# Sample sequences planned four slots ahead of the attention heads, key turns beside the memory jobs

## The reference

```
# prompt: 8 heads of 64, 8 query blocks of 128, keys picked by an indexer (the kernel adds them as a bias)
s = einsum("bthd,btkhd->bthk", q, k_sel) * DH_ATT ** -0.5
p = softmax(where(valid, s, -inf));  o = einsum("bthk,btkhd->bthd", p, v_sel)
# sample: the same for 8 tokens of each of 8 sequences, keys and values from 16 cache pages of 128 rows,
# found by a page table, and from the 8 new tokens
# memory: 4 heads of 128 against 256 memory tokens, for the prompt and for each sample sequence
s = einsum("bthd,bmhd->bthm", qm, mk) * DH_MEM ** -0.5
p = softmax(s);  o = einsum("bthm,bmhd->bthd", p, mv)
```

## Time and profile before

| | |
|---|---|
| time before, median of 3 runs | 3330.24 us (3317.41 to 3333.93) |
| the profiled execution's own time | 3330.28 us |
| span of its trace | 3328.7 us |
| PE busy over the span | 3120.3 us (94%) |
| DVE / ACT / POOL busy | 1747.0 / 914.2 / 669.6 us (52 / 27 / 20%) |
| attention stage in the trace | 1714.5 to 2254.4 us |

### The profile page before, as it was taken

How to read it: one execution, slowest core, us unless ns; L and a number is a source line. 1 busy time by engine, 2 the same in 40 slices (tenths; PEclk the granted TensorE clock), 3 DMA queues, 4 the chain that set the end, 5 groups by cost and what they waited for, 6 DMA issues and landing times. The chain is left out here.

```text
span 3328.7 us, 51750 instructions
## 1 busy us (share of the span) xinstructions
PE 3120.3 (94%) x19690; PEld 2930.0 (88%) x19690; DVE 1747.0 (52%) x3049; ACT 914.2 (27%) x1616; POOL 669.6 (20%) x415
## 2 busy tenths in 40 slices
PE   7999999999998999999778878888999999999999
PEld 7999999999898999899656556567999999999998
DVE  6333333334589999998235555554735333333333
ACT  4111111113333332343334334332132111111111
POOL 2212222213533311233230000002112122222121
PEclk9999999999999999999879999898999999999999
DMA  3111111112222223122543355334431111111111
GB/s 112 45 38 50 44 44 44 44 38 68 73 79 77 79 80 89 39 76 82 165 152 133 115 163 193 115 112 145 153 90 44 40 44 46 43 44 44 44 38 67
DMA packets 256495, 265.47 MB, mean 80 GB/s; under 512 B 14575, under 2 KB 197458, under 8 KB 256334
## 3 DMA queue, kind: packets, MB, share of 16 engines
q1 hardware_dynamic: 250858, 254.61, 24.6%
q0 software_dynamic: 4128, 4.20, 0.4%
q10 hardware_dynamic: 1348, 4.49, 0.4%
HBM read 226.20 MB, written 37.05 MB: 79 GB/s over the span
## 5 line engine op out<-in xcount | busy, mean ns | idle before, releaser
L331 PE MATMUL bank<-h_hi,w_hi 128*128 128x362 f32 (+1 forms) x3384 | 1122.7, 332 | 28.8 <-DVE sg_ffn L513 8.3
L331 PE MATMUL bank<-h_lo,w_hi 128*128 128x362 f32 (+1 forms) x3384 | 1116.3, 330 | 0.0
L331 PE MATMUL bank<-h_hi,w_lo 128*128 128x362 f32 (+1 forms) x3384 | 1112.1, 329 | 0.0
L331 PEld LDWEIGHTS bank<-h_hi,w_hi 128*128 128x128 f32 x3384 | 640.4, 189 | 36.2 <-issue 21.4
L331 PEld LDWEIGHTS bank<-h_lo,w_hi 128*128 128x128 f32 x3384 | 640.9, 189 | 2.8
L331 PEld LDWEIGHTS bank<-h_hi,w_lo 128*128 128x128 f32 x3384 | 641.9, 190 | 0.0
L388 POOL TENSOR_TENSOR w_lo<-raw,w_hi 128x1024 fp32r<-128x1024 f32 x132 | 316.7, 2406 | 1273.3 <-ACT w_hi L483 1273.3
L550 DVE SCALAR_TENSOR_TENSOR x<-bank,x 128x362 f32<-128x362 f32 (+1 forms) x528 | 280.5, 535 | 213.4 <-PE bank L331 213.4
L331 PE MATMUL bank<-a_hi_ffn,w_hi 128*128 128x362 f32 (+1 forms) x1056 | 348.9, 330 | 4.3 <-DVE x L550 2.6
L331 PE MATMUL bank<-a_lo_ffn,w_hi 128*128 128x362 f32 (+1 forms) x1056 | 347.1, 329 | 0.0
L331 PE MATMUL bank<-a_hi_ffn,w_lo 128*128 128x362 f32 (+1 forms) x1056 | 345.7, 327 | 0.0
(11 more groups left out here) (371 smaller groups left out, 4175.6 us busy)
## 6 DMA issues: line engine op xcount, KB each, us to landing
raw<-in_w_ffn_in SPq DMA_DIRECT2D x88, 512.0 KB, 3.8
k_ring<-in_cache_k SPq DMA_DIRECT2D x128, 256.0 KB, 3.9
v_ring<-in_cache_v SPq DMA_DIRECT2D x128, 256.0 KB, 4.1
raw<-in_w_in SPq DMA_DIRECT2D x53, 512.0 KB, 4.9
raw<-in_w_ffn_out SPq DMA_DIRECT2D x44, 512.0 KB, 3.5
kept_g<-stage SPq DMA_DIRECT2D x24, 544.0 KB, 3.1
gate<-kept_g SPq DMA_DIRECT2D x24, 544.0 KB, 3.6
x<-x_kept SPq DMA_DIRECT2D x8, 544.0 KB, 4.6
```

What stands on the lines that cost most here:

```text
L331: mm = pe.matmul(out, left, right, start=(start and i == 0 and j == 0), stop=(stop and i == n - 1 and j == 2))
```

## The change

The sample work of slot k now runs at step k-4, so each sequence starts its slots 0 to 3 beside the four memory jobs of the head before, and the first sequence's slots 0 to 3 run ahead of all heads. The slots are regrouped: `sc 4`, the two memory `kt`, and a new entry `smax` (the maximum over ps, DVE's part of `soft`) stand together in slot 5 and run at step 1; `soft` (now ACT's exponential alone) and `msc` stand in slot 6, step 2. `scale` is gone: the division is folded into the copy of the pv result (`tensor_scalar` instead of `tensor_copy`). `oturn` comes one step later, ahead of the values. SP issues each value page five key pages later than before; its wait for pv and mpv then stands behind six key pages of the next sequence instead of one.

```
--- before.py
+++ after.py
@@ -2321,6 +2321,9 @@
     return cols.rearrange("p (b k) -> p b k", k=LT)[:, :, j]
 
+AHEAD = 4
+
+
 def attention_plan():
 
@@ -2336,9 +2339,9 @@
         [("sc", 0), ("kt", 4), ("kt", 5), ("kt", 6), ("kt", 7)],
         [("sc", 1), ("kt", 8), ("kt", 9), ("kt", 10), ("kt", 11)],
         [("sc", 2), ("kt", 12), ("kt", 13), ("kt", 14), ("kt", 15)],
-        [("sc", 3), ("sc", 4)],
-        [("soft",), ("kt", 16), ("kt", 17)],
-        [("scale",), ("msc",)],
+        [("sc", 3)],
+        [("sc", 4), ("kt", 16), ("kt", 17), ("smax",)],
+        [("soft",), ("msc",)],
         [("pt", 0), ("pt", 1), ("pt", 2), ("pt", 3), ("pt", 4)],
         [("pv",), ("mpt",)],
         [("mpv",), ("ot",)],
@@ -2358,29 +2361,32 @@
     n = len(jobs)
     add("stack", 0)
-    for s in range(n + 2):
-        if s < n:
+    for s in range(-AHEAD, n + 3):
+        if 0 <= s < n:
             add("scores", s)
-        if 0 <= s - 2:
+        if 0 <= s - 3:
+
+            kind, i, h = jobs[s - 3]
+            if kind == "att" and i == 4 and h % 2 == 1:
+                add("oturn", s - 3, 0)
+                add("oturn", s - 3, 1)
+            if kind == "mem" and i % 4 == 3:
+                add("oturn", s - 3, 0)
+        if 0 <= s - 2 < n:
             add("values", s - 2)
-            kind, i, h = jobs[s - 2]
-            if kind == "att" and i == 4 and h % 2 == 1:
-                add("oturn", s - 2, 0)
-                add("oturn", s - 2, 1)
-            if kind == "mem" and i % 4 == 3:
-                add("oturn", s - 2, 0)
         if 0 <= s - 1 < n:
             kind, i, h = jobs[s - 1]
             blocks = i + 1 if kind == "att" else 2
             for g in range(0, blocks, 4):
                 add("turn", s - 1, g, min(4, blocks - g))
-        if s < n:
-
+        if 0 <= s < n:
             add("exp", s)
-            for e in slots[s % 12]:
-                add(e[0], s // 12, *e[1:])
-            if s % 12 == 8 and s // 12 + 1 < H:
-                add("stack", s // 12 + 1)
+        if s + AHEAD < n:
+
+            for e in slots[(s + AHEAD) % 12]:
+                add(e[0], (s + AHEAD) // 12, *e[1:])
+        if s >= 0 and s % 12 == 8 and s // 12 + 1 < H:
+            add("stack", s // 12 + 1)
     return jobs, plan
 
@@ -2441,7 +2447,7 @@
     evicted = [sem("turn_act"), sem("turn_dve")]
     used5, freed5 = sem("used5"), sem("freed5")
-    s_scaled, tail_clear = sem("s_scaled"), sem("tail_clear")
+    tail_clear = sem("tail_clear")
     s_max, s_exp, s_inv, s_norm = sem("s_max"), sem("s_exp"), sem("s_inv"), sem("s_norm")
     m_max, m_exp, m_inv, m_norm = sem("m_max"), sem("m_exp"), sem("m_inv"), sem("m_norm")
@@ -2572,18 +2578,23 @@
                     if u < PAGES:
                         return I[name][0][bass.ds(page(u), 1)].rearrange("a p h d -> p (a h d)")
                     return I[mem_name][0][b].rearrange("(t p) h d -> t p (h d)", p=P)[u - PAGES]
-                for u in range(UP):
+                for u in range(UP + KR - 1):
                     n = b * UP + u
-                    if n >= KR:
-
-                        before = divmod(n - KR, UP)
-                        sp.wait_ge(turned, turn_of[("kt", *before)] + 1)
-                    sp.dma_start(k_ring[:, n % KR, :], source("cache_k", "cache_mem_k", u)).then_inc(k_in[n % KR], 16)
-                    if u == 0 and b >= 1:
+                    if u < UP:
+                        if n >= KR:
+
+                            before = divmod(n - KR, UP)
+                            sp.wait_ge(turned, turn_of[("kt", *before)] + 1)
+                        sp.dma_start(k_ring[:, n % KR, :], source("cache_k", "cache_mem_k", u)
+                                     ).then_inc(k_in[n % KR], 16)
+                    v = u - (KR - 1)
+                    if v < 0:
+                        continue
+                    if v == 0 and b >= 1:
                         sp.wait_ge(used5, use_of[("pv", b - 1)] + 1)
                         sp.wait_ge(used5, use_of[("mpv", b - 1)] + 1)
-                    sp.dma_start(v_ring[:, u, :], source("cache_v", "cache_mem_v", u)).then_inc(v_in[u // 8], 16)
-                    if u == 0:
+                    sp.dma_start(v_ring[:, v, :], source("cache_v", "cache_mem_v", v)).then_inc(v_in[v // 8], 16)
+                    if v == 0:
                         sp.dma_start(vn[:, :], O["new_v_sample"][0][b].rearrange("t h d -> t (h d)")
                                      ).then_inc(vn_in, 16)
@@ -2704,7 +2715,7 @@
                                        stop=(h == 3))
                     mm.then_inc(used5, 1)
                 elif kind == "pt":
-                    pe.wait_ge(s_scaled, s + 1)
+                    pe.wait_ge(s_exp, s + 1)
                     g = entry[2]
                     if g < 4:
                         for q in range(4):
@@ -2794,6 +2805,8 @@
                     act.copy(ps[:, g * 512:g * 512 + w], bank[5][:, 0:w]).then_inc(freed5, 1)
                 elif kind == "soft":
                     act.wait_ge(s_max, s + 1)
+                    if s >= 1:
+                        act.wait_ge(s_inv, s)
                     act.activation(ps[:, :], ps[:, :], ACT.Exp, bias=st[:, 0:1], accum_out=st[:, 1:2]).then_inc(s_exp, 1)
                 elif kind == "msc":
                     act.wait_ge(m_max, s + 1)
@@ -2850,25 +2863,23 @@
                         dve.wait_ge(turned, turn_of[("oturn", last_of["mem", s // 12 - 1], 0)] + 1)
                     dve.tensor_scalar(kept(s), bank[6][:, 0:w], rinv[:, s % 4:s % 4 + 1], None, ALU.mult
                                       ).then_inc(normed, 1)
-                elif kind == "soft":
+                elif kind == "smax":
                     dve.wait_ge(freed5, use_of[("sc", s, 4)] + 1)
                     if s >= 1:
                         dve.wait_ge(s_exp, s)
                     dve.tensor_reduce(st[:, 0:1], ps[:, :], AX.X, ALU.max, negate=True).then_inc(s_max, 1)
-                elif kind == "scale":
-                    dve.wait_ge(s_exp, s + 1)
-                    dve.reciprocal(st[:, 2:3], st[:, 1:2]).then_inc(s_inv, 1)
-                    dve.wait_ge(s_inv, s + 1)
-                    dve.tensor_scalar(ps[:, :], ps[:, :], st[:, 2:3], None, ALU.mult).then_inc(s_scaled, 1)
                 elif kind == "msc":
                     dve.wait_ge(used5, use_of[entry] + 1)
                     dve.tensor_reduce(st[0:32, 3:4], bank[5][0:32, 0:N_MEM], AX.X, ALU.max,
                                       negate=True).then_inc(m_max, 1)
                 elif kind == "pv":
+                    dve.wait_ge(s_exp, s + 1)
+                    dve.reciprocal(st[:, 2:3], st[:, 1:2]).then_inc(s_inv, 1)
+                    dve.wait_ge(s_inv, s + 1)
                     dve.wait_ge(used5, use_of[entry] + 1)
                     if s >= 1:
                         dve.wait_ge(turned, turn_of[("ot", s - 1)] + 1)
-                    dve.tensor_copy(os_[:, :], bank[5][:, 0:P]).then_inc(s_norm, 1)
+                    dve.tensor_scalar(os_[:, :], bank[5][:, 0:P], st[:, 2:3], None, ALU.mult).then_inc(s_norm, 1)
                     dve.wait_ge(s_norm, s + 1)
                     dve.sem_inc(freed5, 1)
                 elif kind == "mpv":
```

## The result

The change makes the kernel faster: 3296.43 us in the median of five runs (3292.73 to 3300.25) against 3325.57 for the kernel before in the same session, a ratio of 0.9915 with an interval of 0.989 to 0.9939. I had forecast 3325, with 0.55 on no change, and the time lies 2.6 us under my lower end of 3299.

The account below looks back on a forecast made before the run. PE's idle time and half clock in the attention stage were taken as the bound. Idle falls from 87 to 71.5 us, gaining 15.5; less 2.7 for the start and 8 for half clock leaves 5 off 3330.28: 3325 us, range 3299 to 3360.

Parts of the forecast that it names:

- What is removed: Attention stage: mks, o_sb, o_m, ps and key page waits go, save 3 us in the start; 64 us if nothing came.
- The stack gap: Steps 8 and 9: PE waits for DVE's copy behind the stack, 3.2 or 3.7 us, plus late exponential; 28 us in all.
- Steps 1 to 3: Copies queue behind the maximum over ps and the exponential; PE idles 21 us in all, against 34 us of old waits.
- steps 6 to 8: These steps lose their sample work; mot waits for a bank and values for a copy, 0.5 us each; 8 us.
- the key turns of step 8: Step 8: the first key turn waits 0.6 us for a copy, the third 0.3; 6 us over seven.
- steps 10 and 11: Key turns in these steps wait 0.35 us each, 5 us in all.
- the end: End of the stage: four last memory jobs with nothing beside them, 3.5 us.
- The start: Sequence 0 turns 16 pages before the first scores, 29.4 us into the stage; 16.6 us lost, a cost of 2.7 us.
- Half clock: PE at half clock behind gaps: 14 us today, 22 after from seven stack gaps and seven small ones; cost 8 us.
- the stack gap is hidden: Faster rival at steps 8 and 9: stack waits of only 1.0 us without loss of clock; 3299 us, chance 0.21.
- The clock halves in steps 8 to 11: Slower rival: old waits mostly stay gone but turns do not keep the clock up, costing 35 us; 3360 us, chance 0.22.
- the 0.8 that I had named: Sign for the half clock rival: mean granted clock below 0.8 in steps 9 to 11.

Follow-up runs that it names:

- e2: The changed kernel with the sample work back at its old steps, no slots ahead; 3254.4 us, 0.9781 of before.
- e10: The kernel before with 11 or 5 useless matmuls of 512 columns added to each mks gap; 3319.7 us, 0.999 of before.
- e11: The kernel of e2 with the stack's differences on GpSimd in place of DVE, as in e3; 3242.3 us, 0.9757 of before.
- e1: The kernel before with only the turns of the results (o_sb, o_m) one step later; 3303.1 us, 0.9929 of before.
- e6: The kernel of e2 with the old grouping of slots 4 to 6; 3293.8 us, 0.9912 of before.
- e12: The changed kernel with the sample work two slots ahead instead of four; 3296.7 us, 0.9925 of before.
- e9: The changed kernel with 14 useless matmuls of 512 columns added to each stack gap; 3290.7 us, 0.9896 of before.
- e3: The changed kernel with the stack's three differences on GpSimd in place of DVE; 3293.5 us, 0.9895 of before.
- e8: The kernel of e3 loading only 128 of 512 columns of each value page from the second sequence on; 3271.1 us, 0.9843 of before.

## Why the prediction was wrong

The stage was to lose 5 us and lost 27.9. By the steps of the prediction:

- **What is removed** came as said. The mks, o_sb, o_m and ps waits are gone from the top of the list (1.7 us and less are left of each), and page waits behind the first page are 2.5 us, for the 3 or so that I had left.
- **The stack gap** is where the prediction put it, in seven heads, and of the size it gave for the bank alone: 3.18 us in each even head and 3.96 in each odd one, 4 x 3.18 + 3 x 3.96 = 24.6 us, for 28 predicted. What did not come are the 0.3 and 0.9 us that I added for the late exponential.
- **Steps 1 to 3**: 21 us predicted, 15.1 measured. A stretch of the timeline of after, in an odd head:

```profile
1804.57 0.66 PE L2680 MATMUL bank<-ident,o_m 128*128 128x128 f32 x4 [0.42 <-DVE mks L2523]
...
1804.81 2.29 DVE L2870 TENSOR_REDUCE st<-ps 128x1 f32<-128x2056 f32 x1 [0.29 <-ACT ps L2805]
...
1807.55 0.68 DVE L2509 COPY qmT<-bank 128x512 f32<-128x512 f32 x1
...
1808.29 0.66 PE L2655 MATMUL bank<-ident,pb 128*128 128x128 f32 x4 [2.31 <-DVE qmT L2509]
```

  The maximum over ps does hold the copy of the o_m turn, as said, and PE waits 2.31 us for it (2.6 predicted), but the smaller waits around it are 0.42 and 0.20, not 1.35. In even heads it is 0.81, not 1.5.
- **The rest**: steps 6 to 8 8.2 us (8 predicted), the key turns of step 8 6.3 (6), steps 10 and 11 about 5 (5), the end 2.1 (3.5). With the above this is 61 to 64 us, by whether steps 1 to 3 and the smallest waits are counted by head or by group, for 71.5. The working was right and rounded up in many places, all to the same side: the gain in idle time is 23 to 26 us, not 15.5 (by the windows, idle time behind the start fell from 89.5 to 65.5 us), so **about 8 us of the miss** lie here.
- **The start**: the first scores begin 29.2 us into the stage (29.4 predicted). With the 12.8 us of work that I had counted, 16.4 us are lost (16.6); the windows give the same, 9.9 us of idle time and 6.4 of half clock, for 9.5 and 3.4 in the first 20 us of before. Cost 2.5 to 3.4 us for 2.7.
- **Half clock** is the term that was mis-sized most. I put before's at 14 us and after's at 22. After's is 22.0. Before's is 22.2, by the same sum over stretches of 2 us. The step that failed is the count of today's half clock: I had counted only spells right behind gaps that I had looked at, from the turns that follow them, and had not seen that msc and mpv run at half clock in most heads. The earlier trace rows said so, with 543 ns a matmul where e2 has 382. **The change therefore costs no clock behind the start, and 8 us of the miss** are this one term. Nor does the cost go by the number of gaps: in e10's trace the mks gaps are filled and it is only 1.0 us lower.
- **What is left**, 27.9 - 5 - 8 - 8 = 7 us, is in part PE's busy time without the half clock, start included, which I held constant: 415 us in before, 409.5 in after, 411 in e2. In after the missing records can be the reason for most of it; e2 has all its records, and there 4 us stay. The rest is what the sums over many small rows round away. What makes PE's own work shorter stays open.

The profiled run of before, 3330.28 us, is also at the slow end: in later sessions before's median was 3322 to 3326. My time was made against it, so 4 to 5 us of the distance from 3325 to 3296 are there and not in the sum.

**Of the rivals**, *the stack gap is hidden* gave nearly the right time, 3299, for a reason that did not occur: the gap is there at 24.6 us. *The clock halves in steps 8 to 11* did not occur as it stood. The last row of the windows of after, 20 us of head 6 with its key turns and memory jobs, is at 1.00, but that is the best head. Steps 9 to 11 of heads 0 and 4:

```profile
1777.44:1797.97 20.53, 16.32 (x117) 10.63 (x116) 11.61 (x23) 10.24 (x20) 0.00 (x0) 0.92 0.86 282
...
2028.79:2049.00 20.21, 16.44 (x112) 10.80 (x110) 10.92 (x22) 10.24 (x20) 0.00 (x0) 0.83 0.84 267
```

Over seven heads the mean is 0.89 and no head is below the 0.8 that I had named: the clock falls for a part of these steps, and does not stay down. The Trainium skill (TensorE: Matmul & The Clock Gate, Part 4: PE-mode transpose) says that turns in transpose mode do not count as activity for the clock. No run here bears that out: with the same turns, e11 is at 1.00 over 432 us of the stage.

**What I did not ask** is which part of the change the gain comes from. By the ratios, in one chain: the results turned a step later bring 24 us (before to e1), the new order of the transfers and the folded division 6 more (to e6; within the noise), the regrouping 44 (to e2), and running four slots ahead, which the change is named for, takes 45 back (to after). The prediction had read rightly that the mks wait goes because the maximum stands behind the memory turns in the plan. What hid the rest was to add up the change only as a whole: that the same new order holds without running ahead (the mks wait is gone in e2 and e12 too), and what it would be worth there, was not asked. What the move does, as I read it, is to take the sample's PE work out of steps 6 to 8 and to put the key turns, which want a copy and a page every 0.72 us (half of the 1.44 of the earlier trace rows), where DVE has the stack to do.

## What to carry to other kernels

Take a change apart in the prediction as you would in an experiment: give each part its own sum against the kernel without it, since a large gain (39 us here, e6 to e2) and a large loss (42, e2 to after) can stand in one diff and each look like the other's condition. Count today's half-clock time from rows of the whole stage (a mean duration far above the shortest of the same form shows it at once), before you charge a change for new spells. When a gap is removed, look at what landed in it: with the stack on GpSimd some 24 us of gaps went and 3 us came out; 15.5 us of the rest came back as page waits.

## What the runs showed of the hardware

- **A small DVE instruction waits for GpSimd's.** A one-column `tensor_tensor` of 0.16 us took 1.91 us beside a GpSimd `tensor_tensor` of 2.35 us, and the mean of 96 rose from 160 to 238 ns (e2 to e11). The Trainium skill, SBUF — State Buffer, Who interferes with whom, says that an instruction of DVE with two inputs in SBUF, as this one, and one of GpSimd shut each other out of a shared pair of ports for their whole length; the trace agrees. Even so the move gained 12 us (e2 to e11; 8 by the ratios).
- **The half clock moves.** Filling eight gaps changed the clock's cost by 1.0 us (e10), filling seven others by 10.1 (e9), in one trace each; behind the start it vanished only in e11, with the stack off DVE and 1.3 us of page waits. A price per gap, as I used, does not hold.
- **fp32 matmuls of 256 columns** (128 x 32 stationary) take 382 ns in the mean in e2 and e10, the shortest 379. In before they take from 379 to 636, so the mean of 543 is one of both levels of the clock.
- **Bytes set when a page lands, not how often pages are issued.** A key and a value page, 512 KB, were issued every 1.57 us. With a quarter of the value columns the pace stayed at 1.58, the median time of a key page from issue to landing fell from 4.2 to 2.8 us, and page waits from 18.0 to 7.3 us (e3 to e8).
